# Neighborhood attention in a chained block kernel: query tiles of 16 grid columns with 192 or 256 local keys in place of tiles of 2 grid rows with 512

## The reference

```
def neighborhood_attention(q, k, v, kc, vc, rpb):
    rows = L // GRID_W                       # 8
    kh, kw = min(NA_KH, rows), min(NA_KW, GRID_W)     # 8, 16
    col_start = jnp.clip(cols - kw // 2, 0, GRID_W - kw)
...
        r0 = jnp.clip(r - kh // 2, 0, rows - kh)       # always 0 here
        s_loc = einsum(q_row, k_win) * scale + rpb[:, row_off, col_off]
        s_ctx = einsum(q_row, kc) * scale
        p = softmax(concatenate([s_loc, s_ctx]))
        return einsum(p_loc, v_win) + einsum(p_ctx, vc)
```

## Time and profile before

| | |
|---|---|
| time, median of 3 runs | 2878.23 us (2877.51 to 2887.64) |
| profiled execution | 2878.87 us, of which the span of its profile is 2877.1 |
| PE busy | 2738.0 us, 95% of the span |
| DVE, ACT, POOL busy | 1314.2, 1097.8, 859.5 us |
| groups of the stage | from the first scores at 92.36 us to the last near y_lo at 571 to 572 us |
| PE busy from 100 to 580 us | 453.39 of 480 us |
| weight loads of 1 MB, issue to landing | 4.8 us median |

### The profile page before, as it was taken

The page is one execution under the profiler, slowest core; times in us unless marked ns, Lnnn a source line. Parts: engine busy times, 40 slices in busy tenths (PEclk is TensorE's granted clock), DMA queues, the critical chain, the costliest instruction groups (busy, mean ns, idle before and its releaser), DMA issues. The chain is left out here.

```text
span 2877.1 us, 40246 instructions
## 1 busy us (share of the span) xinstructions
PE 2738.0 (95%) x16006; PEld 2223.1 (77%) x16006; DVE 1314.2 (46%) x2489; ACT 1097.8 (38%) x1854; POOL 859.5 (30%) x656
## 2 busy tenths in 40 slices
PE   5899999899999999999989999999999999899997
PEld 3777877778888888766657787777777888698886
DVE  4335343553333335546564444554444344505544
ACT  3444444441122222455553222344443433442222
POOL 1202111023223323111114444423324343245444
PEclk9999999999999999999999999999999999999999
DMA  6222333211211111222212222221212122122221
GB/s 232 89 90 101 122 110 107 95 45 59 71 60 58 59 72 37 77 88 89 89 45 79 97 89 101 73 92 59 74 59 96 59 74 77 71 89 88 95 96 59
DMA packets 58630, 238.92 MB, mean 83 GB/s; under 512 B 4468, under 2 KB 28532, under 8 KB 34296
## 3 DMA queue, kind: packets, MB, share of 16 engines
q1 hardware_dynamic: 58488, 236.94, 23.3%
HBM read 234.83 MB, written 2.10 MB: 82 GB/s over the span
## 5 line engine op out<-in xcount | busy, mean ns | idle before, releaser
L245 POOL TENSOR_TENSOR w_lo<-w_raw,w_hi 128x512 fp32r<-128x512 f32 x622 | 813.4, 1340 | 1921.1 <-ACT w_hi L238 631.7
L284 PE MATMUL bank<-u_hi,w_hi 128*128 128x512 f32 (+1 forms) x1984 | 743.9, 375 | 18.4 <-POOL w_lo L245 10.7
L286 PE MATMUL bank<-u_hi,w_lo 128*128 128x512 f32 (+1 forms) x1984 | 731.8, 369 | 0.0
L285 PE MATMUL bank<-u_lo,w_hi 128*128 128x512 f32 (+1 forms) x1984 | 731.4, 369 | 0.0
L284 PEld LDWEIGHTS bank<-u_hi,w_hi 128*128 128x128 f32 x1984 | 376.1, 190 | 96.5 <-issue 18.7
L285 PEld LDWEIGHTS bank<-u_lo,w_hi 128*128 128x128 f32 x1984 | 376.2, 190 | 62.7 <-issue 2.0
L286 PEld LDWEIGHTS bank<-u_hi,w_lo 128*128 128x128 f32 x1984 | 375.3, 189 | 63.3
L859 DVE SCALAR_TENSOR_TENSOR resid<-bank,mod,resid 128x512 f32<-128x512 f32 (+1 forms) x384 | 242.3, 659 | 163.9 <-PE bank L286 161.9
L284 PE MATMUL bank<-hid_hi,w_hi 128*128 128x512 f32 (+1 forms) x768 | 278.0, 362 | 4.2 <-DVE resid L859 4.1
L286 PE MATMUL bank<-hid_hi,w_lo 128*128 128x512 f32 (+1 forms) x768 | 273.6, 356 | 0.0
L285 PE MATMUL bank<-hid_lo,w_hi 128*128 128x512 f32 (+1 forms) x768 | 272.6, 355 | 0.0
(11 more groups left out here) (381 smaller groups left out, 3949.9 us busy)
## 6 DMA issues: line engine op xcount, KB each, us to landing
w_raw<-stream SPq DMA_DIRECT2D x184, 1024.0 KB, 4.8
w_raw<-stream SPq DMA_DIRECT2D x44, 512.0 KB, 4.5
ada_more<-stream SPq DMA_DIRECT2D x4, 1024.0 KB, 10.9
bias<-bias SPq DMA_DIRECT2D x16, 256.0 KB, 5.5
resid<-h SPq DMA_DIRECT2D x1, 3072.0 KB, 10.2
bias<-bias SPq DMA_DIRECT2D x8, 384.0 KB, 5.4
out<-resid SPq DMA_DIRECT2D x8, 256.0 KB, 2.0
w_raw<-stream SPq DMA_DIRECT2D x4, 256.0 KB, 4.6
```

What stands on the lines that cost most here:

```text
L245: ins = eng.tensor_tensor(m.wl[:, s, w], m.raw[:, s, w], m.wh[:, s, w].bitcast(F32), ALU.subtract)
L284: pe.matmul(out, lh, rh, start=start, stop=False)
L285: pe.matmul(out, lh, rl, start=False, stop=False)
L286: return pe.matmul(out, ll, rh, start=False, stop=stop)
```

## The change

Inside the stage the 512 tokens now lie column by column: token index = 8 * column + row. A near tile of 128 queries is then 16 grid columns with all 8 rows, and its keys are the 24, 32, 32 or 24 columns of `NA_KEYS`, that is 192, 256, 256 or 192 local keys for t = 0 to 3. The far group stays as it was. In detail:

- `Apply` writes its scratch tile with a step of 8 elements (32 bytes) for the 8 items of 512 tokens; everything projected from `u_hi` and `u_lo` is then in the new order.
- `high_y` and `low_y` of near groups read PSUM with a step of 8 elements and write 8 runs of 16 elements, which restores the row-major order.
- Scores, bias, exponentials, `e` and `pt` shrink from 512 to at most 256 local columns. A group uses two PSUM banks (one for each head: local and context side by side) instead of three. The separate wait for the first context product is gone.
- `v` tiles are kept shifted by 64 tokens where a query tile needs keys from the middle of a token tile. `values` therefore takes three instructions for each of its first two parts instead of one, and two of the four query tiles use a block of only 64 keys.
- The bias is kept in three blocks (`t` = 1 and 2 share one), [128, 2, 3, 512] instead of [128, 2, 896]. The DRAM layout is as before, so each block is loaded by 8 DMAs, one for each grid row, of 16 partitions, 2 heads and 2 KB: 24 DMAs for a pair instead of 3.

```
-        bias = sb("bias", [P, 2, 14 * GRID_W])
-        s_sb = sb("s", [P, 2, LAT])
-        e = sb("e", [P, 2, TOK])
-        pt = sb("pt", [P, 3, LAT])
+        bias = sb("bias", [P, 2, 3, LAT])
+        s_sb = sb("s", [P, 2, LOC])
+        e = sb("e", [P, 2, LOC + CTX])
+        pt = sb("pt", [P, 2, LOC + CTX])
...
+            if self.by_columns and w == 0:
+                out, h, rstd = columns_as_rows(out), grid(h), grid(rstd)
...
+        WHOLE, UPPER, LOWER = slice(0, P), slice(0, DH), slice(DH, P)
+        LOCAL = (((64, 128), 3, UPPER), ((128, 256), 0, WHOLE)), (((0, 128), 0, WHOLE), ((128, 256), 1, WHOLE)), (
+            ((0, 128), 1, WHOLE), ((128, 256), 2, WHOLE)), (((64, 192), 2, WHOLE), ((128, 256), 3, LOWER))
...
+                def load_bias(i, block, done):
+                    for r in range(GRID_H):
+
+                        c, o = ((0, 6 - r) if r < 7 else (GRID_W, 0))
+                        c, o = c + (0, 16, 48)[block], o * GRID_W
+                        sp.dma_start(bias[r:P:GRID_H, :, block, :],
+                                     m.in_bias[2 * i:2 * i + 2, c:c + 16, o:o + LAT].rearrange(
+                                         "h p w -> p h w")).then_inc(done.sem, 16)
...
                     if t == 2 and i + 1 < PAIRS:
                         sp.wait_ge(*max_parts.at(NEAR * i + 3))
-                        load_bias(i + 1, RIGHT, bias_in)
+                        load_bias(i + 1, 0, bias_in)
+                        load_bias(i + 1, 1, bias_in)
                     if t == 3 and i + 1 < PAIRS:
                         sp.wait_ge(*max_parts.at(NEAR * i + 4))
-                        load_bias(i + 1, MIDDLE, bias_in)
-                        load_bias(i + 1, LEFT, bias_left_in)
+                        load_bias(i + 1, 2, bias_last_in)
...
+                    if p == 0:
+                        act.activation(to[UPPER, 0:2, :], out[LOWER, :, :], ACT.Copy)
+                        act.activation(to[UPPER, 3, :], out[UPPER, 0, :], ACT.Copy)
+                        ins = act.activation(to[LOWER, 0, :], out[UPPER, 1, :], ACT.Copy)
...
-                    b = 3 if t < NEAR else 2
-                    act.activation(pt[:, 0:b, :], banks(G)[:, 0:b, :], ACT.Copy).then_inc(copied.sem)
+                    act.activation(pt[:, :, :], banks(G), ACT.Copy).then_inc(copied.sem)
...
+                        ins = act.activation(grid(yh[:, i % 4, 0:LAT])[:, :, 16 * t:16 * t + 16],
+                                             columns_as_rows(banks(G)[:, 0, 0:P]), ACT.Copy)
...
+                        a, b = (GRID_H * x for x in NA_KEYS[t])
+                        for o, keys in ((local(t), slice(a, b)), (slice(LOC, LOC + CTX), slice(LAT, TOK))):
+                            for hd in range(2):
+                                r = half(hd)
+                                ins = pe.matmul(s[:, hd, o], q[r, c], k[r, keys], start=True, stop=True)
...
+                            for b, ((x, y), _, _) in enumerate(LOCAL[t]):
+                                pe.transpose(s[0:y - x, hd, b * P:b * P + P], e[:, hd, x:y], cst(m, "ident"))
+                            for x in (LOC, LOC + P):
+                                ins = pe.transpose(s[:, hd, x:x + P], e[:, hd, x:x + P], cst(m, "ident"))
...
+                        for b, (tile, keys) in enumerate(blocks):
+                            for hd in range(2):
+                                r = half(hd)
+                                ins = pe.matmul(s[r, 0, 0:P], vp[keys, tile, r], pt[keys, hd, b * P:b * P + P],
+                                                start=(b == 0), stop=(b == 3))
```

More of the change, by code:

```diff
@@ L27 @@
 NA_KH, NA_KW = 8, 16
+GRID_H, LOC = 8, 256
+NA_KEYS = (0, 24), (8, 40), (24, 56), (40, 64)
 CHUNK = 2048
@@ L1211, in banks, with local, bias_of, by_columns @@
         def banks(G):
-            return m.bank[:, 2 + 3 * (G % 2):5 + 3 * (G % 2), :]
+            return m.bank[:, 2 + 2 * (G % 2):4 + 2 * (G % 2), :]
         def half(hd):
             return slice(DH * hd, DH * hd + DH)
-        LEFT, MIDDLE, RIGHT = slice(0, 256), slice(256, 512), slice(512, 14 * GRID_W)
-        def bias_of(t):
-            o = (6 - 2 * t) * GRID_W
-            return slice(o, o + LAT)
+        WHOLE, UPPER, LOWER = slice(0, P), slice(0, DH), slice(DH, P)
+        LOCAL = (((64, 128), 3, UPPER), ((128, 256), 0, WHOLE)), (((0, 128), 0, WHOLE), ((128, 256), 1, WHOLE)), (
+            ((0, 128), 1, WHOLE), ((128, 256), 2, WHOLE)), (((64, 192), 2, WHOLE), ((128, 256), 3, LOWER))
+        def local(t):
+            a, b = NA_KEYS[t]
+            return slice(LOC - GRID_H * (b - a), LOC)
+        def bias_of(hd, t):
+            a, b = NA_KEYS[1 if t == 2 else t]
+            return bias[:, hd, (0, 1, 1, 2)[t], :].rearrange("p (r c) -> p c r", c=GRID_W)[:, a:b, :]
+        def by_columns(x):
+            return x.rearrange("p (c r) -> p c r", r=GRID_H)
         ada_landed = {}
@@ L1338, in exps @@
                         for hd in range(2):
-                            act.activation(e[:, hd, 0:LAT], s_sb[:, hd, :], ACT.Exp, bias=st[:, 4 + hd:5 + hd],
-                                           accum_out=st[:, 8 + hd:9 + hd])
+                            act.activation(e[:, hd, local(t)], s_sb[:, hd, local(t)], ACT.Exp,
+                                           bias=st[:, 4 + hd:5 + hd], accum_out=st[:, 8 + hd:9 + hd])
                         for hd in range(2):
-                            ins = act.activation(e[:, hd, LAT:TOK], s[:, 2, hd * CTX:hd * CTX + CTX], ACT.Exp,
+                            ins = act.activation(e[:, hd, LOC:LOC + CTX], s[:, hd, LOC:LOC + CTX], ACT.Exp,
                                                  bias=st[:, 4 + hd:5 + hd], accum_out=st[:, 10 + hd:11 + hd])
@@ L1464, in normalise @@
                         for hd in range(2):
-                            ins = dve.tensor_scalar(e[:, hd, :], e[:, hd, :], st[:, 12 + hd:13 + hd], None, ALU.mult)
+                            x = e[:, hd, local(t).start:LOC + CTX]
+                            ins = dve.tensor_scalar(x, x, st[:, 12 + hd:13 + hd], None, ALU.mult)
                     else:
@@ L1670, in weigh @@
                         pe.wait_ge(*lin.read(use["vv", i // 2, 2]))
-                    for b in range(6 if t < NEAR else 2):
-                        for hd in range(2):
-                            r = half(hd)
-                            if t == NEAR:
-                                ins = pe.matmul(s[r, 2, 0:CTX], vp[:, 4 + b, r], pt[:, hd, b * CTX:b * CTX + CTX],
+                    if t < NEAR:
+                        blocks = [(tile, keys) for _, tile, keys in LOCAL[t]] + [(4, WHOLE), (5, WHOLE)]
+                        for b, (tile, keys) in enumerate(blocks):
[3 more added lines that the diff above has]
+                                                start=(b == 0), stop=(b == 3))
+                    else:
+                        for b in range(2):
+                            for hd in range(2):
+                                r = half(hd)
+                                ins = pe.matmul(s[r, 0, 0:CTX], vp[:, 4 + b, r], pt[:, hd, b * CTX:b * CTX + CTX],
                                                 start=(b == 0), stop=(b == 1))
-                            else:
-                                p = pt[:, hd, b * P:b * P + P] if b < 4 else pt[
-                                    :, 2, hd * CTX + (b - 4) * P:hd * CTX + (b - 3) * P]
-                                ins = pe.matmul(s[r, 0, 0:P], vp[:, b, r], p, start=(b == 0), stop=(b == 5))
                     ins.then_inc(weighed.sem)
```

71 lines of the change are left out of this document (35 added, 36 removed).

## The result

The changed kernel takes 2852.37 us in the median of 4 runs (2850.3 to 2852.72), the one before on the same chip 2880.26 (2877.51 to 2887.64). The ratio is 0.9889, with a 95% interval of 0.9873 to 0.9904: 1.1% faster, 28 us. The profiled execution took 2852.7 us, 26.2 less than the one of before. The forecast of 39 us less had the direction and the mechanism of the main term right, and was 1.4 times the 28 us measured. The time lies inside the range.

A forecast was written before the change was run, and what follows sets the result against it. PE, busy 2738.0 of 2877.1 us, was taken to bound the kernel. Terms -46.4 + 5.3 + 3.0 - 2.6 + 0.7 + 1.0 = -39.0 us gave 2839 us, range 2828 to 2857.

The forecast's parts named there:

- What comes off PE: In the 32 near groups, shorter scores (15.2 us), transposes (15.6) and weighing (15.6) take 46.4 us off PE.
- Tile shapes: Near transposes and weighing on PE: six extra tile-shape changes a pair at 0.11 us, +5.3 us over 8 pairs.
- rival 3: Gain larger than counted: no drain for 64-high blocks (-5.3 us), one or two half-clock stretches less; 2830 us, chance 0.10.
- values on ACT: ACT's split copies of v end later than y_high would start: 0.12 us at six places, +0.7 us.
- DVE's gates: Where PE waits for DVE's chain from y_low to the transposes, part of the saving is lost: +3.0 us.
- waits for ACT: In pairs 0 and 6, shorter copies and exponentials on ACT bring y_high earlier; with the first group, -2.6 us.
- Steps of 32 bytes: Stepped accesses by DVE and ACT (Apply, y_high, y_low, bias) cost almost nothing: +1 us taken, range 0 to +9.
- rival 1: DVE and ACT pay per element at steps of 32 bytes or more: 2847 us, 2856 at triple time; chance 0.15.
- The upper bound's price for the Apply passes: At the head, time per column doubles in 8 stepped DVE passes on the chain PE waits for: +4.2 us.
- rival 2: Work hiding the chain shrinks, waits replace it and PE's clock halves for stretches: 2850 to 2854 us; chance 0.12.
- rival 4: Sixteen bias issues above 0.9 us each on SP's queue delay the next weights; 2907 us at 1.5 each, chance 0.03.
- The test that the prediction set itself: Prediction wrong if the stage's end does not move by 33 to 45 us, or time is lost behind the stage.

The follow-up runs named there:

- apply_plain: Changed kernel with Apply writing its scratch tile without a step, so tokens keep row order and the output differs; 2849.1 us.
- cols_in: Changed kernel with a second, column-ordered copy of the input, so Apply needs no step; residual rows loaded over it later, function kept; 2840.54 us.
- after_third: Changed kernel, no edit, traced a third time; 2846.76 us.
- before_again: The kernel before the change, unedited, traced once more; 2881.1 us.
- bias_3dma: Changed kernel with 3 bias DMAs a pair of 128 partitions in place of 24 of 16 (other data loaded); 2856.57 us.
- after_again: Changed kernel, no edit, traced a second time; 2856.6 us.
- warm_stage: Changed kernel with 16 dummy products where PE waits: 4 ahead of the first head sums, 12 in pairs 0, 6 and 7; 2840.82 us.
- cols_warm: Changed kernel with column-ordered input plus dummy products in prologue and stage waits; median 2839.74 us, ratio 0.9845 to the kernel before.

## Why the prediction was right, and where its sizes were not

- **What comes off PE** (-46.4): the mechanism was right, the size some 3 us too large. Scores are on the forecast to 0.01 us; transposes at 1.02 and the weighing at 1.02 to 1.03 lie 0.04 to 0.05 above 0.98, which is those 3 us over 32 groups.
- **Tile shapes** (+5.3): the term was mis-sized. Three of the six changes a pair, those of the alternating transposes, show no cost, against the prediction's sentence that the extra changes cost what any change costs (in part rival 3); the three of the weighing cost 0.43 us a pair where nothing covers them (pairs 2 and 4), 0.15 each and not 0.11, and 0.14 a pair beside ACT's copies. That is 1.3 us in these five pairs, and at the same rates an estimated 2 in all.
- **values on ACT** (+0.7): the mechanism was right, ACT's copies are in front of y_high. The size was 0.43 a pair in three pairs, 1.3 us. With the term above, 5.3 + 0.7 = 6.0 us stood in the sum and about 3.3 were measured; the 3 us too many taken off PE make up for the difference. That the steady pairs landed on 4.7 us is thus partly luck: errors of 3 us each way cancel.
- **DVE's gates** (+3.0) and **waits for ACT** (-2.6): not isolated. The steady pairs, whose sum holds the first, came out at 4.63 to 4.89 against 4.7. Pair 0, which holds a half of the second, gained 4.84 although its low clock lasted 6.8 us in place of 3.4.
- **Steps of 32 bytes** (+1 of 0 to 9): this step failed. I went by the absence of a row. The head alone lost 3.4 us, shown by apply_plain and cols_in: rival 1 came true for DVE's passes at the head. The upper bound's price for the Apply passes (4.2 us) is near these 3.4, but by another sum: 1.9 us of longer chain and 1.5 of clock, which it did not count. The price for y_high and y_low (5 us) was not borne out at all, and ACT's part of rival 1 neither. The Trainium skill, Advanced Engine Details and Errata, Memory Cachelines, gives SBUF lines of 16 bytes, with a penalty where each access goes to a different one. By that rule DVE's passes at 32 and 256 bytes in SBUF had to be slower, and the trace agrees (1.17 against 0.74 us, 601 against 417 ns). Of its PSUM lines of 8 bytes the section says that non-contiguous access slows matmuls; the prediction carried this over to ACT's and DVE's reads, and for their 128 columns the trace shows no penalty (278 against 279 ns, 291 against 292).
- **Waits and clock** (rival 2): held to be 12% likely as the sole story, it came as a part. From 60 us on the stage has 27.2 us at the low level in place of 13.6 in the two profiled executions (17.1 in after_third, 13.6 in before_again), and filling the waits gave back 1.5 us in the head and 2.0 to 4.25 in the groups. Its mechanism (steps that hid the chain become shorter, the wait stays) is that of pairs 0, 6 and 7; in the head it is the longer wait behind DVE.
- **The DMA queue** (rival 4): excluded by bias_3dma, though an issue cost 0.67 us, not 0.44, and the margin is 2.1 us. At the head the 24 issues took 15.6 us, not 14.
- **The test that the prediction set itself** (the stage's end moves by 33 to 45 us) failed in the profiled execution: the last y_lo came 578.59 - 550.46 = 28.1 us earlier. In after_third it was 35.5, inside; between before_again and after_again 26.9. So by this test of its own the prediction failed, and it is met only with after_third, whose start is as early as that of the kernel before.

The sum in the rows of the two executions: forecast -39.0; ahead of the stage +4.5; head +3.4 against the +1 counted, 2.4 more; behind the stage +1.9; this makes -30.2. The measured -26.2 is 4.0 us short of it, and these lie in the groups: -36.0 measured from first scores to last y_lo, -40.0 forecast. after_third, with 10 us less at the low level and no edit, is 2.25 us shorter there than after, and warm_stage, with no low stretch, 4.25. But the kernel before had low stretches in its groups too, and pair 6, in which the modulation piece waits 2.08 us in place of 0.89, gains nothing from the dummies beyond after_third. So an exact split of these 4 us between clock, the late DMA piece in pair 6 and the small excess of the transposes isn't to be had from these runs.

What stays open: why the clock is up by 31 to 33 us in some executions and rises only at 57.7 to 58.0 in others; and whether the kernel before ever starts late. If it does so as often as the changed one, the 4.5 us of the prologue are no cost of the change, and the medians are that much less apart by chance.

## What to carry to other kernels

When a layout is changed so that later steps shrink, price the pass that makes the layout as if each element cost nearly twice (here 0.8 ns more for each column, on some 1.05), and look for a place where it can be had for nothing, such as the order in which the input is stored. Work taken off the bounding engine pays fully only where other work follows at once. Where a wait follows, the wait stays, and the shorter work around it can also drop the engine's clock; a few dummy products there gave 3.5 to 5.7 us, by the execution that they are held against. Where there is no wait they cost time (0.6 us in the head of cols_warm). Compare landmarks inside the traces before single times: here unchanged code moved by 5 us ahead of the stage and by 6 behind it.

## What the runs showed of the hardware that was not expected

- A DVE pass of 512 columns whose SBUF output steps by 32 bytes takes 1.16 to 1.17 us, unstepped 0.74. One whose bias operand in SBUF steps by 256 bytes takes 601 ns for 256 columns; unstepped, and under another instruction name, 417. Reads of PSUM in steps of 32 bytes, 128 columns, cost ACT and DVE nothing (278 and 291 ns).
- Transposes that alternate between 64 and 128 columns of weights show no price for it (0.99 us for eight, 1.02 without the change); in the weighing, each change between 64*64 and 128*64 costs about 0.15 us (1.17 in place of 1.02 us with one, 2.19 in place of 1.89 with two).
- A DMA of 16 partitions with 2 heads of 2 KB holds SP's queue for 0.63 to 0.67 us in the stage; the larger ones of before took 0.44 to 0.48.
- The same PE prologue ran at the high clock level from 31 to 33 us on until 38 to 41 in 8 of 12 traces and stayed at the low one until 57.7 to 58.0 in 4, with the first Apply pass 5 us apart.
